# Fourteen groups of context value rows gathered in the experts' first rounds, and a stage border with loads on both sides of it

## The chip, the cores and the metric

One core of one Trainium2 chip runs the whole program as one launch. The metric is the device time of the launch in microseconds (us), the median of several runs. Its engines run side by side and are named as in the profile: PE (TensorE, matrix products; PEld are its weight loads), DVE (VectorE), ACT (ScalarE), POOL (GpSimd, which here mostly issues gathers), and SP (SyncE, which issues the plain transfers). They meet only in semaphores.

## The reference, cut to what matters

One layer of a backbone for 1024 latent tokens and 256 context tokens of width 1024: a mixing half (projection, attention, a gated linear recurrence, output projection), then a product-key expert half, then a norm. The change is in the expert half:

```python
def peer_ffn(x, w_q, sub_keys, u, v):
    q = (x @ w_q).reshape(N, PEER_HEADS, 2, PEER_D_HALF)
    s = jnp.einsum('nhpd,pkd->nhpk', q, sub_keys)
    s_top, i_top = lax.top_k(s, PEER_TOPK)            # 16 of 128, twice per head
    ...                                               # top 16 of the 256 sums, softmax g
    act = jax.nn.gelu(jnp.einsum('cd,ced->ce', x_c, u[e_c]))   # 128 experts per token
    return jnp.einsum('ce,ced->cd', g_c * act, v[e_c])
```

Each token picks 128 of 16384 experts; an expert is one row of u (its key) and one row of v (its value), 4 KB each.

## The kernel before

**Stages.** Tokens are handled in tiles of 128: 8 latent, 2 context. Four latent tiles (the dense tiles) go through all 16384 experts by matrix products. The other four latent tiles and the two context tiles are gathered: for every one of a tile's 128 slots, an indirect DMA from POOL brings one u row per token (128 rows, 512 KB) and DVE takes its dot product with the token; then for every token, the 128 v rows of its slots are gathered and PE sums them with the weights. Four tokens make a *value group*: four gathers of 512 KB and eight products [32 columns of weights x 512] into one PSUM tile; a tile has 32 groups.

The order is: context tiles through mixing and routing; latent mixing, with the context tiles' key dots beside it; **latent routing** (`routing`, names `route_lat_*`), which computes scores and top-k for the 8 latent tiles and has all 64 context value groups beside it (`val_*`); **placing** (`place_weights`), which builds the dense tiles' weight matrix g, token by expert, tile by tile in two SBUF grids of 8 MB and stores each to HBM; the **experts** (`experts`, names `exp_*`); the final norm. Every stage is one block: all engines meet at its end, and the next stage's buffers take the place of the old ones.

**Latent routing.** PE runs over 4 weight slabs x 2 chunks of 512 tokens; a chunk is 4 column tiles of 8 x 2 products, then 16 x 2 short products for the scores of its 4 units. A value group stands after every half column tile (`values(1)`, twice per `ct`), in PE's program order. DVE takes two units at a time in `turn(unit)`, 16 turns; the line that starts a turn's decoding of the last one is L1592. POOL does per two units: `pick` (L1562, a product of 128x1024) and one group of gathers, twice, then `steps` and two groups: four groups, 16 gathers, per turn. Both lists of groups are in POOL's and PE's program order, so a late gather holds all that follows. After the last turn PE turns the gathered tiles' activations (`h_ps`, the PSUM tile the value groups use), ACT stores them, then takes the exponential of the weights (L1528), and DVE norms them (L1734 to L1739).

**Placing.** DVE compares indices with an iota, PE multiplies the one-hot pairs, ACT writes the grid; SP stores each tile's grid when it is full (L1877) and the block ends when the last store has landed. 32 of the first gathered latent tile's key dots stand beside it.

**Experts.** 64 rounds of 2 expert rows: SP loads u (512 KB), v (512 KB) and g (256 KB) for each; ACT and DVE split them in high and low halves; PE makes `a_ps` (48 products of 128x512), then for the round before `o_ps` (48 products), which DVE adds to `acc`. Beside it the four gathered latent tiles: rounds 0 to 7 ("keys") have 12 key gathers each, rounds 8 to 55 ("both") 8 key gathers and 8 value gathers (2 groups), rounds 56 to 63 ("values") 16 value gathers. Key rows sit in a ring of 4, value rows in a ring of two groups. On POOL the gathers alternate, and each waits for its place in the ring. At a tile's end ACT copies the sums out and SP stores them (`finish`). Before round 0 the stage loads h2T (2 MB) and the first two u, and splits them.

**How DVE's round is ordered** (it sets the round's pace where the dots are many):

```python
add_tile(2, DENSE_TILES - 2)
factors(); DOT()
add_tile(2, DENSE_TILES - 1)
factors_turned()
spread()
DOT(); split_v(0)
...
DOT(); add_tile(1, 0); DOT(); add_tile(1, 1)
```

`split_v(0)` waits for v's high half from ACT, and so for the load of v.

## Time and profile before

| | us |
|---|---|
| median of 3 runs | 3849.93 |
| lowest and highest of them | 3842.12, 6262.26 |
| the profiled execution's own time | 3871.46 |
| its span, first to last instruction | 3869.7 |
| latent routing in it, from 1119.7 to 1610.3 | 490.6 |
| placing, from 1610.3 to the last store's issue at 1834.05 | 223.8 |
| that store, to the next stage's first instruction at 1864.89 | 30.8 |
| experts, to 3811; final norm, to 3869.7 | 1946; 58.7 |

Over the span PE is busy 82%, DVE 68%, POOL 52%, ACT 27%; the 16 DMA engines moved 1137.52 MB, 294 GB/s on the mean. Times of a stretch are read from the start of the span. A matrix product of fp32 operands stands as two records in the latent routing's rows. A PE product's duration holds its pipeline's latency, so the spacing of products is less than their duration.

### The profile page before, as it was taken

What the parts mean: (1) busy time and instruction counts of PE and PEld (TensorE: products, weight loads), DVE (VectorE), ACT (ScalarE), POOL (GpSimd) and SP (SyncE); (2) the same over time, 40 slices, a digit from 0 to 9 for tenths busy, and PEclk for the clock granted to TensorE, in tenths of its full rate; (3) what the DMA queues carried; (4) which work ended last, traced back from release to release, by engine and by line L of the source; (5) the groups of instructions that cost most, each with busy time, mean ns of one, the idle gap of its engine ahead of it and who ended that gap; (6) DMA issues with size and microseconds to landing.
All of it is one profiled execution on the core that took longest, in us unless ns stands there. A gap on an engine that the chain in (4) does not pass through costs nothing. (4 is left out here: it accounts for less than half of the span.)

```text
span 3869.7 us, 47496 instructions
## 1 busy us (share of the span) xinstructions
PE 3181.5 (82%) x15280; PEld 2098.8 (54%) x15280; DVE 2635.3 (68%) x5937; ACT 1043.0 (27%) x1811; POOL 2012.7 (52%) x1765
## 2 busy tenths in 40 slices
PE   5776799698969888577377899998999899999993
PEld 3546345465433333366266666666666666666662
DVE  2227687697457777799488777767777777775445
ACT  4431044365110010266222222222222222222221
POOL 0001455354237888421345677767677677775450
PEclk8888899899979999688688999999999999999996
DMA  6522677666578988566887999999999999999996
GB/s 252 183 82 89 229 247 251 189 226 229 207 254 307 330 310 305 195 203 202 302 284 268 387 391 388 382 348 397 370 380 379 372 376 387 384 389 343 343 352 247
DMA packets 412569, 1137.52 MB, mean 294 GB/s; under 512 B 33937, under 2 KB 129425, under 8 KB 412177
## 3 DMA queue, kind: packets, MB, share of 16 engines
q0 software_dynamic: 221184, 805.40, 57.1%
q1 hardware_dynamic: 191248, 330.43, 24.0%
q8 instruction: 69, 1.13, 0.1%
q14 instruction: 68, 0.55, 0.0%
HBM read 1080.13 MB, written 55.58 MB: 293 GB/s over the span
## 5 line engine op out<-in xcount | busy, mean ns | idle before, releaser
L2195 POOL DMA_INDIRECT exp_key_row<-in_u_rows,exp_u_id x480 | 598.2, 1246 | 328.2 <-DVE exp_dot L2249 154.5
L2203 POOL DMA_INDIRECT exp_value_row<-in_v_rows,exp_v_id x512 | 576.6, 1126 | 343.1 <-issue 165.2
L2249 DVE CUSTOM_DVE_ANT_0 exp_key_row<-exp_key_row,exp_x 128x1024 f32<-128x1024 f32 x480 | 585.0, 1222 | 189.4 <-DMA exp_key_row<-in_u_rows,exp_u_id 156.3
L358 POOL DMA_INDIRECT ahead_row<-in_u_rows,keep_expert_id x256 | 328.5, 1283 | 370.7 <-DVE keep_dot L368 309.7
L2112 PE MATMUL exp_o_ps<-exp_v_hi,exp_w_hi 128*128 128x512 f32 x1024 | 346.6, 421 | 160.7 <-DVE exp_acc L2312 153.0
L2097 PE MATMUL exp_a_ps<-exp_xT_hi,exp_u_hi 128*128 128x512 f32 x1024 | 411.5, 402 | 56.8 <-DVE exp_xT_lo L2227 50.5
L2312 DVE TENSOR_TENSOR exp_acc<-exp_o_ps,exp_acc 128x1024 f32<-128x1024 f32 x256 | 311.4, 1222 | 147.7 <-PE exp_o_ps L2112 129.1
L2097 PE MATMUL exp_a_ps<-exp_xT_lo,exp_u_hi 128*128 128x512 f32 x1024 | 404.1, 395 | 0.0
L2097 PE MATMUL exp_a_ps<-exp_xT_hi,exp_u_lo 128*128 128x512 f32 x1024 | 402.0, 393 | 0.0
L368 DVE CUSTOM_DVE_ANT_0 ahead_row<-ahead_row,ahead_x 128x1024 f32<-128x1024 f32 x256 | 304.2, 1221 | 70.1 <-DMA ahead_row<-in_u_rows,keep_expert_id 66.1
L2112 PEld LDWEIGHTS exp_o_ps<-exp_v_hi,exp_w_hi 128*128 128x128 f32 x1024 | 197.4, 201 | 265.7 <-DVE exp_acc L2312 204.0
L434 POOL DMA_INDIRECT val_row<-in_v_rows,keep_value_id x256 | 273.6, 1069 | 115.2 <-issue 68.8
L2112 PE MATMUL exp_o_ps<-exp_v_lo,exp_w_hi 128*128 128x512 f32 x1024 | 333.2, 408 | 0.0
L2112 PE MATMUL exp_o_ps<-exp_v_hi,exp_w_lo 128*128 128x512 f32 x1024 | 331.1, 406 | 0.0
L2097 PEld LDWEIGHTS exp_a_ps<-exp_xT_hi,exp_u_hi 128*128 128x128 f32 x1024 | 194.5, 190 | 148.6 <-DVE exp_xT_lo L2227 50.7
L2083 PE MATMUL exp_v_ps<-exp_value_row,exp_hot 128*32 128x512 f32 x2048 | 248.8, 598 | 10.1 <-DMA exp_value_row<-in_v_rows,exp_v_id 9.5
L1454 PE MATMUL route_lat_q_ps<-mix_featT,route_lat_slab 128*128 128x512 f32 x512 | 238.4, 611 | 2.0 <-DMA route_lat_slab<-in_w_q 2.0
L617 PE MATMUL proj_lat_ps<-mix_featT,proj_lat_slab 128*128 128x512 f32 x512 | 224.9, 598 | 11.0 <-DMA proj_lat_slab<-in_w_in 11.0
L2148 ACT ACTIVATE exp_v_hi<-exp_v_raw 128x1024 fp32r<-128x1024 f32 x128 | 135.0, 1055 | 365.4 <-PE exp_o_ps L2112 214.3
L2112 PEld LDWEIGHTS exp_o_ps<-exp_v_lo,exp_w_hi 128*128 128x128 f32 x1024 | 203.6, 199 | 46.4
L2112 PEld LDWEIGHTS exp_o_ps<-exp_v_hi,exp_w_lo 128*128 128x128 f32 x1024 | 202.9, 198 | 45.6
L2151 ACT ACTIVATE exp_hidden<-exp_a_ps 128x512 f32<-128x512 f32 x128 | 76.5, 598 | 547.5 <-PE exp_a_ps L2097 409.4
(376 smaller groups left out, 5188.1 us busy)
## 6 DMA issues: line engine op xcount, KB each, us to landing
exp_u_raw<-in_uT SPq DMA_DIRECT2D x130, 512.0 KB
exp_v_raw<-in_v_rows SPq DMA_DIRECT2D x128, 512.0 KB
scratch_g<-place_grid SPq DMA_DIRECT2D x4, 8192.0 KB, 35.8
exp_g_raw<-scratch_g SPq DMA_DIRECT2D x128, 256.0 KB
proj_ctx_mod_slab<-in_w_mod SPq DMA_DIRECT2D x8, 2048.0 KB, 14.4
proj_ctx_slab<-in_w_in SPq DMA_DIRECT2D x10, 1024.0 KB, 5.1
proj_lat_slab<-in_w_in SPq DMA_DIRECT2D x10, 1024.0 KB, 7.9
mod_slab<-in_w_mod SPq DMA_DIRECT2D x4, 2048.0 KB, 19.4
```

What stands on the lines that cost most here:

```text
L358: nc.gpsimd.indirect_dma_start(out=ahead.row[:, n % KEY_RING, :], out_offset=None, in_=io["u_rows"], in_offset=bass.IndirectOffsetOnAxis(a ...
L368: nc.vector.tensor_tensor_reduce(out=row, in0=row, in1=ahead.x[:, n // SLOTS - ahead.first, :], scale=1.0, scalar=0.0, op0=ALU.mult, op1=A ...
L434: nc.gpsimd.indirect_dma_start(out=val.row[:, 4 * slot + t, :], out_offset=None, in_=io["v_rows"].rearrange("a b n -> (a b) n"), in_offset ...
L617: last = nc.tensor.matmul(ps[C * (ct % 2) + c][:, 0:width], slab[ct // 2][:, k, ct % 2 * P:(ct % 2 + 1) * P], hT[:, k, g.at + at:g.at + at ...
L1454: last = nc.tensor.matmul(q_ps[ct][:, 0:width], slab[:, a % 2, k, ct * P:(ct + 1) * P], h2T[:, k, g.at + at:g.at + at + width], start=(k = ...
L2083: mm = nc.tensor.matmul(v_ps[QUAD * t:QUAD * (t + 1), half * SLAB:(half + 1) * SLAB], hot[:, i % 2, t, :], value_row[:, 4 * (i % 2) + t, h ...
L2097: mm = nc.tensor.matmul(a_ps[e][:, :], u[part][:, e, k, :], xT[xp][:, k, :], start=(k == 0 and part == 0 and xp == 0), stop=(k == KD - 1 a ...
L2112: mm = nc.tensor.matmul(o_ps[t % 2][:, c, :], w[part][:, 1 - parity, e, t * P:(t + 1) * P], v[xp][:, 1 - parity, e, c * SLAB:(c + 1) * SLA ...
L2195: nc.gpsimd.indirect_dma_start(out=key_row[:, j % RING, :], out_offset=None, in_=io["u_rows"], in_offset=bass.IndirectOffsetOnAxis(ap=u_id ...
L2203: nc.gpsimd.indirect_dma_start(out=value_row[:, 4 * (j % 2) + t, :], out_offset=None, in_=io["v_rows"].rearrange("a b n -> (a b) n"), in_o ...
L2249: nc.vector.tensor_tensor_reduce(out=key_row[:, j % RING, :], in0=key_row[:, j % RING, :], in1=x[:, :], scale=1.0, scalar=0.0, op0=ALU.mul ...
L2312: nc.vector.tensor_tensor(acc[:, t, :], o_ps[t % 2][:, :, :].rearrange("p c n -> p (c n)"), acc[:, t, :], ALU.add).then_inc(added, 1)
```

## The change

Fourteen of the 64 context value groups (the last 14 of the second context tile) leave latent routing and are gathered and summed in the experts' rounds 1 to 7, two per round, where "keys" rounds had no values; POOL's list there becomes key, value, key, value, key, key, value and so on. The context tile's weights stay in `keep["share"]`; at round 1 PE turns them, and after round 7 a new `finish(-1)` copies the sums out and stores the 56 rows.

The border between placing and experts changes too. `acc` becomes a lasting buffer, so that h2T can be loaded into it during placing; x and the first two u are loaded at placing's start; the last grid's store is split into its first 4 expert rows (`g_first`) and the other 124 (`g_rest`), and the block of placing no longer waits for either. SP waits for `g_first` before the first g load, and every engine that writes a buffer lying over the second grid waits for `g_rest` at round 1. Other buffers (routing's rest, two of attention's, the norm's squares, the routes) move onto `acc`; their instructions stay as they are.

```diff
+FIRST_KEYS = 4
+LATE_GROUPS = 14
 class Values:
+        self.units = [(k, q) for k in range(CONTEXT_GATHER) for q in range(self.GROUPS)]
+        del self.units[-LATE_GROUPS:]
 def factor_weigh(nc, keep, val, dve, k):
-    nc.vector.tensor_tensor(val.factor[:, k, :], val.act[:, :], keep["share"][:, k * SLOTS:(k + 1) * SLOTS], ALU.mult)\
+    share = keep["share"][:, k * SLOTS:(k + 1) * SLOTS]
+    nc.vector.tensor_tensor(share, val.act[:, :], share, ALU.mult)\
 def routing(...):  (on PE and on POOL)
-            values_left = [(k, q) for k in range(CONTEXT_GATHER) for q in range(val.GROUPS)] if val else []
+            values_left = list(val.units) if val else []
 def place_weights(nc, io, keep, scratch, routes, ahead, edge):
         def _(sp):
-            sp.dma_start(ahead.x[:, 0, :], scratch["h2"][0]).then_inc(x_in, 16)
+            sp.dma_start(ahead.x[:, 0, :], scratch["h2"][0]).then_inc(edge.x_in, 16)
+            for n in range(2):
+                sp.dma_start(edge.u_raw[:, n, :, :], io["uT"][n]).then_inc(edge.u_in[n], 16)
+            sp.wait_ge(turned, DENSE_TILES)
+            sp.dma_start(keep["acc"][:, :, :].rearrange("p t n -> p (t n)").rearrange("p (k n) -> p k n", k=KD),
+                         scratch["h2T"]).then_inc(edge.h2_in, 16)
-            for t in range(DENSE_TILES):
+            for t in range(DENSE_TILES - 1):
                 sp.wait_ge(placed, (t + 1) * PER_TILE)
                 sp.dma_start(place[:, :, t * P:(t + 1) * P], grid[t % 2][:, :, :]).then_inc(stored[t % 2], 16)
-            for j in range(2):
-                sp.wait_ge(stored[j], 16 * (DENSE_TILES // 2))
+            last = slice((DENSE_TILES - 1) * P, DENSE_TILES * P)
+            sp.wait_ge(placed, DENSE_TILES * PER_TILE)
+            sp.dma_start(place[:, 0:FIRST_KEYS, last], grid[1][:, 0:FIRST_KEYS, :]).then_inc(edge.g_first, 16)
+            sp.dma_start(place[:, FIRST_KEYS:N_KEYS, last], grid[1][:, FIRST_KEYS:N_KEYS, :]).then_inc(edge.g_rest, 16)
+            sp.wait_ge(stored[0], 32)
+            sp.wait_ge(stored[1], 16)
 def experts(nc, io, keep, scratch, ahead, edge):
             with engine.Fori(1, FIRST // 2) as i:
-                body(2 * i, 0, "keys", None, None)
-                body(2 * i + 1, 1, "keys", None, None)
+                body(2 * i, 0, "keys", None, 2 * i + FIRST)
+                body(2 * i + 1, 1, "keys", None, 2 * i + 1 + FIRST)
+            finish(-1)
         def value_groups(r, mode):
-            if mode == "both":
-                return [2 * r - 2 * FIRST + i for i in range(2)]
+            if mode in ("keys", "both") and at_least(r, 1):
+                return [2 * r - 2 + i for i in range(2)]
         def _(sp):
-            sp.dma_start(h2T, scratch["h2T"]).then_inc(h2_in, 16)
...
-            load_u(0, 0)
-            load_u(1, 1)
...
                         sp.wait_ge(weighted, n - 1)
+                    else:
+                        sp.wait_ge(edge.g_first, 16)
+                    if isinstance(r, int) and r == 1:
+                        sp.wait_ge(edge.g_rest, 16)
             def finish(k):
-                sp.wait_ge(out_ready, k + 2)
+                sp.wait_ge(out_ready, k + 3)
+                if isinstance(k, int) and k < 0:
+                    for t in range(4):
+                        rows = slice(QUAD * (t + 1) - LATE_GROUPS, QUAD * (t + 1))
+                        sp.dma_start(scratch["ffn"][CTX.first + 1][rows, :], out[rows, :]).then_inc(late_stored, 16)
         def _(pe):
+                late_tile = mode == "keys" and isinstance(r, int) and r == 1
+                if late_tile:
+                    nc.tensor.transpose(v_ps[:, 0:P], keep["share"][:, SLOTS:2 * SLOTS], keep["ident"][:, :])\
+                      .then_inc(factor_turned, 1)
         (on ACT, POOL and DVE, at the head of their round 1)
+                if isinstance(r, int) and r == 1:
+                    act.wait_ge(edge.g_rest, 16)
         def _(pool):
-                if keys and groups:
-                    moves = [x for pair in zip([("key", j, n, 0) for j, n in enumerate(keys)], moves) for x in pair]
+                for j, n in enumerate(keys):
+                    moves.append(("key", j, n, 0))
+                    if len(keys) == len(values) or j % 3 != 2:
+                        moves += values[0:1]
+                        del values[0:1]
+                moves += values
```

## Rows read from the trace of the kernel before

**Rows 1.** Windows: latent routing, placing, the last store, the experts' start.

```profile
core 0: us, PE busy (x) PEld busy (x) DVE busy (x) ACT busy (x) POOL busy (x), PEclk, DMA share, GB/s
1119.70:1610.30 490.60, 410.14 (x1830) 166.28 (x1830) 329.18 (x1857) 48.85 (x78) 361.57 (x336) 0.92 0.85 298
1610.30:1834.05 223.75, 160.73 (x1036) 153.48 (x1036) 218.02 (x464) 150.72 (x384) 50.75 (x32) 0.83 0.63 191
1834.05:1864.89 30.84, 0.00 (x0) 0.00 (x0) 0.00 (x0) 0.00 (x0) 0.00 (x0) 0.57 0.90 272
```

**Rows 2.** Who waited for whom in latent routing: us, times, longest.

```profile
PE route_lat_h_ps L448 <- DMA val_row<-in_v_rows,keep_value_id: 58.9, 31, 4.9
DVE routes_first L1585 <- POOL route_lat_hit L1562: 48.2, 16, 4.8
```

**Rows 3.** Costliest groups of instructions on POOL in latent routing.

```profile
L434 POOL DMA_INDIRECT val_row<-in_v_rows,keep_value_id x256 | 273.6, 1069 | 115.2 <-issue 68.8 <-PE route_lat_h_ps L448 35.8 <-POOLq L101 8.7
L1562 POOL TENSOR_TENSOR route_lat_hit<-route_lat_hit,route_lat_key_step 128x1024 f32<-128x1024 f32 x32 | 75.8, 2369 | 5.0 <-DVEq L1716 4.5
```

**Rows 4.** Timeline of DVE: the decoding line of turns 12 and 14 and of the tail.

```profile
1481.13 0.18 DVE L1592 TENSOR_SCALAR route_lat_region<-route_lat_best_at 128x64 uint32<-128x64 uint32 x1
...
1536.84 0.18 DVE L1592 TENSOR_SCALAR route_lat_region<-route_lat_best_at 128x64 uint32<-128x64 uint32 x1
...
1585.72 0.20 DVE L1592 TENSOR_SCALAR route_lat_region<-route_lat_best_at 128x64 uint32<-128x64 uint32 x1
```

**Rows 5.** Timeline of PE: the last chunk's first products, one group, its scores.

```profile
1482.83 3.60 PE L1454 MATMUL route_lat_q_ps<-mix_featT,route_lat_slab 128*128 128x512 f32 x8
1486.35 1.95 PE L448 MATMUL route_lat_h_ps<-val_row,val_spread 128*32 128x512 f32 x16
1534.81 3.90 PE L1470 MATMUL route_lat_s_ps<-route_lat_keysT,route_lat_qT 128*128 128x128 f32 x32
```

**Rows 6.** Timeline of the last steps of latent routing and the first of placing.

```profile
1604.02 1.28 ACT L1528 ACT_TABLE_LOAD   x1
1606.40 1.22 DVE L1734 TENSOR_REDUCE route_lat_norm<-routes_weight 128x64 f32<-128x1024 f32 x1 [9.07 <-ACT routes_weight L1528]
1610.47 0.23 DVE L1792 COPY place_mine<-routes_first 128x128 f32<-128x128 f32 x1 [0.54 <-PEq L101]
```

**Rows 7.** Timeline around the border of placing and experts.

```profile
1834.05 0.37 SPq L1877 DMA_DIRECT2D scratch_g<-place_grid  x1
1864.89 0.19 POOL L2178 COPY exp_u_id<-keep_expert_id 128x12 int32<-128x12 int32 x1 [59.63 <-POOLq L101]
1876.75 1.06 ACT L2130 ACTIVATE exp_u_hi<-exp_u_raw 128x1024 fp32r<-128x1024 f32 x1 [42.73 <-DMA exp_u_raw<-in_uT]
1889.33 1.23 DVE L2249 CUSTOM_DVE_ANT_0 exp_key_row<-exp_key_row,exp_x 128x1024 f32<-128x1024 f32 x1
1891.62 1.22 DVE L2219 TENSOR_TENSOR exp_v_lo<-exp_v_raw,exp_v_hi 128x1024 fp32r<-128x1024 f32 x1
```

**Rows 8.** DMA issues: count, KB each, median us from issue to landing.

```profile
scratch_g<-place_grid SPq DMA_DIRECT2D x4, 8192.0 KB, 35.8
route_lat_keysT<-in_keysT SPq DMA_DIRECT2D x1, 128.0 KB, 17.6
```

**Rows 9.** Windows of the experts: rounds 3 to 5, round 8, rounds 9 to 22.

```profile
1987.23:2080.49 93.26, 72.02 (x290) 58.10 (x289) 77.23 (x109) 19.75 (x27) 47.53 (x40) 0.89 0.82 287
2144.31:2177.67 33.36, 27.89 (x130) 20.16 (x129) 21.90 (x30) 6.71 (x9) 21.17 (x20) 0.90 1.03 407
2177.67:2579.82 402.15, 377.11 (x1794) 270.97 (x1793) 303.68 (x420) 90.34 (x126) 290.58 (x253) 0.97 1.00 383
```

**Rows 10.** Key gathers in rounds 3 to 5; value products in rounds 11 and 12.

```profile
L2195 POOL DMA_INDIRECT exp_key_row<-in_u_rows,exp_u_id x37 | 46.9, 1269 | 46.8 <-DVE exp_dot L2249 40.2 <-issue 4.0 <-POOL exp_u_id L2178 2.7
L2083 PE MATMUL exp_v_ps<-exp_value_row,exp_hot 128*32 128x512 f32 x64 | 7.8, 598 | 0.0
```

**Rows 11.** Windows: rounds 7 to 9 and rounds 23 to 25, each with a tile's end.

```profile
2113.39:2203.71 90.32, 78.49 (x355) 58.73 (x354) 69.58 (x100) 19.76 (x27) 62.09 (x53) 0.92 0.96 363
2579.82:2670.78 90.96, 82.25 (x387) 59.44 (x386) 65.27 (x92) 20.42 (x28) 59.01 (x52) 0.94 0.96 363
```

More of the change, by code:

```diff
@@ L351, in hold, with __init__ @@
         self.first = first
+class Edge:
+    def __init__(self, scope, signals):
+        self.u_raw = scope.sb("u_raw", [P, 2, KD, P])
+        self.u_id = scope.sb("u_id", [P, 2, KEYS_PER_ROUND], I32)
+        self.dot = scope.sb("dot", [P, 2, KEYS_PER_ROUND])
+        self.act_row = scope.sb("act_row", [P, SLOTS])
+        self.h2_in = signals.sem("edge_h2_in")
+        self.u_in = [signals.sem(f"edge_u_in{n}") for n in range(2)]
+        self.x_in = signals.sem("edge_x_in")
+        self.g_first = signals.sem("edge_g_first")
+        self.g_rest = signals.sem("edge_g_rest")
 def gather_keys(nc, io, ahead, pool, n):
@@ L414, in factor_turn @@
     pe.wait_ge(val.factor_ready, k + 1)
[L415 removed]
+    nc.tensor.transpose(ps[:, 0:P], keep["share"][:, k * SLOTS:(k + 1) * SLOTS], keep["ident"][:, :])\
+      .then_inc(val.turned, 1)
 def factor_spread(nc, val, act, k, ps):
@@ L1362, in routing @@
         score = s.sb("score", [P, SCORE_RING, 4, N_KEYS])
-        rest = s.sb("rest", [P, 2, 4, N_KEYS])
+        rest = keep["acc"][:, 3, :].rearrange("p (x c n) -> p x c n", x=2, c=4)
         top = s.sb("top", [P, 2, 4, TOPK])
@@ L1536, in _ @@
         def _(pool):
-            values_left = [(k, q) for k in range(CONTEXT_GATHER) for q in range(val.GROUPS)] if val else []
+            values_left = list(val.units) if val else []
             def values(count):
@@ L1740, in _, with place_weights @@
             c.wait()
-def place_weights(nc, io, keep, scratch, routes, ahead):
+def place_weights(nc, io, keep, scratch, routes, ahead, edge):
     first, second, weight = routes
@@ L1929, in experts @@
         zeroed = s.sem("zeroed")
-        u_in = [s.sem(f"u_in{n}") for n in range(2)]
+        u_in = edge.u_in
         v_in = [s.sem(f"v_in{n}") for n in range(2)]
@@ L2029, in load_u @@
                 sp.dma_start(u_raw[:, e, :, :], io["uT"][n]).then_inc(u_in[e], 16)
-            load_u(0, 0)
-            load_u(1, 1)
             def body(r, parity, mode, tile, _):
-                if tile is not None and mode in ("keys", "both"):
-                    if mode == "both":
-                        sp.wait_ge(dots, SLOTS * tile + RING)
-                    sp.dma_start(x[:, :], scratch["h2"][tile]).then_inc(x_in, 16)
+                if tile is not None and mode == "both":
+                    sp.wait_ge(dots, SLOTS * tile + RING)
+                    sp.dma_start(x, scratch["h2"][tile]).then_inc(x_in, 16)
                 if mode == "end":
@@ L2174, in body @@
                     return
+                if isinstance(r, int) and r == 1:
+                    pool.wait_ge(edge.g_rest, 16)
                 c = Chain(pool, own_pool)
@@ L2180, in body @@
                 if groups:
-                    c.step(nc.gpsimd.tensor_copy(v_id[:, parity, 0:4 * len(groups)],
-                                                 keep["value_id"][:, bass.ds(4 * groups[0] + BASE, 4 * len(groups))]))
+                    c.step(nc.gpsimd.tensor_copy(
+                        v_id[:, parity, 0:4 * len(groups)],
+                        keep["value_id"][:, bass.ds(4 * groups[0] + BASE - 4 * LATE_GROUPS, 4 * len(groups))]))
                 c.wait()
@@ L2237, in body @@
                 new_tile = tile is not None and (not isinstance(tile, int) or tile) and mode != "end"
+                late_tile = mode == "keys" and isinstance(r, int) and r == 1
                 last = mode == "end"
@@ L2272, in spread @@
                     i, m = groups.pop(0)
-                    per = 2 if mode == "both" else 4
+                    per = 4 if mode == "values" else 2
                     q = per * local + i
                     if new_tile and i == 0:
-                        dve.wait_ge(factorT_ready, tile)
+                        dve.wait_ge(factorT_ready, tile + 1)
+                    if late_tile and i == 0:
+                        dve.wait_ge(factorT_ready, 1)
                     dve.wait_ge(values_done, m + 1)
@@ L2313, in add_tile @@
                                                 acc[:, t, :], ALU.add).then_inc(added, 1)
+                if isinstance(r, int) and r == 1:
+                    dve.wait_ge(edge.g_rest, 16)
                 DOT = dot_product
@@ L2467, in program @@
+        with Scope(nc, "edge") as e:
+            edge = Edge(e, s)
+            ahead.hold(e, CONTEXT_GATHER, 1)
+            place_weights(nc, io, keep, scratch, routes, ahead, edge)
+            experts(nc, io, keep, scratch, ahead, edge)
         final_norm(nc, io, scratch)
```

156 lines of the change are left out of this document (78 added, 78 removed).

## The prediction

> **What bounds the kernel now.** I read first the windows by stage, then within a stage who waits for whom, then the timeline at the places the change touches. The chain that ended last covers only the final norm and says nothing here.
>
> In latent routing no engine is full: PE 410, POOL 362, DVE 329 of 490.6 us [rows 1]. The reader is to see that POOL's time is larger than its busy share. A gather is 1.07 us and another 0.30 of issue gap (68.8 us in 228 waits) [rows 3]. Per turn that is 16 x 1.37 = 21.9, two picks of 2.37, and about 1.1 of small steps: 27.7 us, against two turns in 55.7 us (1481.13 to 1536.84) [rows 4]. So POOL's gathers set the pace; PE waits 58.9 us for value rows in its program order, and DVE waits 48.2 us for picks that stand behind gathers [rows 2]. Placing is DVE alone, 218 of 223.75 us [rows 1]. Then all five engines rest 30.8 us for one store [rows 1], and another 24.4 us pass until the first key dot at 1889.33 [rows 7]. In the experts' keys rounds (31.1 us each) DVE is busy 25.7 us, DMA 0.82 at 287 GB/s; in the both rounds (28.7 us each) DMA is full, 1.00 at 383 GB/s [rows 9]. The keys rounds are thus the ones with room, but not much.
>
> **Latent routing: -30 us.** Groups go out three ahead and four per turn, so 50 groups end in turn 11 (3 + 4 x 12 = 51). PE takes 8 per chunk in chunks 1 to 6 and the last 2 in chunk 7, so up to 1481 nothing changes. From turn 12 on POOL has only picks. DVE's busy time is 329/16 = 20.6 us per turn; I take 20.7 with no wait for POOL. PE must deliver the last chunk in time: 8 x 3.6 + 2 x 1.95 = 32.7 us from 1482.83 [rows 5], so its scores come at about 1517 instead of 1536, while DVE wants them at 1481.1 + 41.4 = 1522.5. PE is no longer late. Four turns take 82.8 instead of 104.6 us (1481.13 to 1585.72) [rows 4]: -21.8. At the end, PE's value groups and the transposes behind them no longer hold ACT until 1604.02: DVE waited 9.07 us for ACT's exponential [rows 6]; what stays of it is a table load of 1.28 and the exponential of 1.1 behind DVE's last weights, of which DVE covers 1.5 with the ids. -8. Together -30, range -24 (some POOL wait stays, PE at a lower clock) to -33. Late next is DVE itself. The removed PE products, 14 x 1.95 us, lay in the same wait and are not counted twice.
>
> **Placing: 0.** Three loads more on SP's queue (3 MB) and the gathers of the first key rows meet in its first 15 us; DVE is the bound and reaches its first dot 10 us in. If the first row came late it would cost up to 3 us once. The second store of a tile is another 0.37 us on SP. The end wait is for stores that were issued a whole tile earlier (56 us; a store takes 35.8 [rows 8]), so it is free.
>
> **The border: -23 us.** Experts start about 1 us after 1834.4 instead of at 1864.89. u and h2T are there, so ACT splits at 1835.5 instead of 1876.75, and DVE reaches its first dot 12.6 us later, as before [rows 7]: 1848 for 1889.33, which would be -41. But DVE's third step is split_v, and v's load is issued by SP behind the 7.75 MB of g_rest. Do loads of one queue go past each other? The nearest row: keysT, 128 KB, landed 17.6 us after its issue with 2 MB of slabs issued just before it on the same queue [rows 8]. So I take it that they don't. The store takes 30.8 to 35.8 us in this kernel [rows 1, 8], the four key rows (2.1 MB) share its engines; v lands at about 1869.5, DVE goes on at 1871 for 1891.62: -21, and its key rows wait ready, which saves 2 more. The waits for g_rest at round 1 are by then met. Behind the waiting DVE stand dots, and POOL's ring of 4 waits for them; PE has done both first `a_ps` and waits for the next u, also in that queue. Ends: -15 if the key rows take half the engines' time for long, -41 if v comes past.
> The Trainium skill says in "DMA: Bandwidth & Descriptors", section "Queues, rings and completion order", that an engine consumes a ring's descriptors in order and goes round between the queues by packets. By that rule the SP loads stay behind the store and only POOL's gathers come through; the trace's 17.6 us agree, and the sum stays at -23.
>
> **Rounds 1 to 7: +21 us.** Per round are added 8 gathers of 512 KB, two weight builds on DVE (under 1 us), and two groups on PE (7.8/4 = 1.95 us each) [rows 10]. PE and DVE have it free: 25.7 + 0.7 us of DVE, 24 + 3.9 of PE. The round's bytes grow from 8.5 to 12.5 MiB = 13.1 MB. At the 383 GB/s of the full rounds that is 34.2 us against 31.1: +3.1, times 7 = +21. POOL's queue is near: 20 gathers at 1.269 + 0.30 is 31.4, with copies and their waits 34. Ends: round 8 shows 407 GB/s [rows 9], so 32.2 us, +8; with waits of POOL for value places, 37 us, +40.
> The Trainium skill, same page, section "Where 436 GB/s comes from", gives about 358 GB/s as what binds a core's traffic with HBM. By it a round would be 36.6 us and this term +38, the whole -11. Here the trace differs: 383 GB/s over 402 us [rows 9], so the sum goes by the row.
>
> **The tile's end at round 8: +4 us.** finish(-1) puts before SP's loads of round 8 a wait for ACT's copy, which waits for PE's last value group, at the end of PE's round. Queued behind it are x, v, g and u of round 8. Before, SP waited there for the dots only. Rounds 7 to 9 took 90.3 us; rounds 23 to 25, with such a finish, 91.0 [rows 11], where three both rounds are 86.1: +4.9 for a full tile's end, against 90.3 - (31.1 + 57.4) = 1.8 now. +3, and a little for a queue fuller than at 23; ends 0 and +11 (how much later PE's last group is than the last dot). Rounds 8 to 63 keep their work: 0. The final norm: 0; the context rows are there earlier than it needs them.
>
> **Sum.** -30 - 23 + 21 + 4 = -28 against the profiled execution's own 3871.5: 3843.5. That execution is 21.5 us above the median of 3849.9; taken over to it, 3822. Two per cent is 77 us, about what a measurement of this kernel can tell from no change: the case is small against it.
>
> **The rivals.**
> *Value gathers make POOL's list the bound of the keys rounds.* A value gather waits for its ring place, which PE frees only in its `o_ps` phase; keys for DVE's dots stand behind it, DVE runs dry. For it: 34 us of POOL in a 34 us round, and POOL's and DMA's limits meet. Against: in both rounds the same alternation holds 28.7 us with DMA full. With two waits of 2.7 us in a round 39.3 us: +57, the tile's end +11; -30 - 23 + 68 = +15, 3865, slower than before. It decides from a round of 38 us (49 us in 7 rounds).
> *The loads come past the store.* Round 0 runs at once, -41 for -23: 3804. For it: nothing in the rows; against: the 17.6 us.
> *The rounds absorb the gathers* at 32.2 us: +8 for +21: 3809.
> *The rounds move their bytes at a lower rate* than the full rounds, 36.6 us each: +38 for +21, 3839. Against: the full rounds' 383 GB/s [rows 9]. The 358 GB/s of the Trainium skill's page, cited above, would do this.
> *The routing gains only its tail*, DVE's turns staying at the 27 us of now because picks or scores bind otherwise: -8 for -30, 3844. Against: 48.2 us of waits for POOL.
>
> **How the numbers follow.** Forecast 0.5, POOL's list 0.12, loads past the store 0.08, absorbed 0.16, lower rate 0.06, routing tail 0.08. The range takes in the absorbed rounds with part of the border's better end, and up to near the first rival: 3790 to 3858. Faster by over 2% (under 3773) needs all good ends and more: 0.04. Slower by over 2% (over 3927) needs a rival of twice its price: 0.02.
>
> **What would show it.** Value gathers on POOL end near turn 11; L1592's last four spacings near 21 us; placing starts 30 us earlier and lasts 224 us. The last store is followed at once by experts; ACT's first v split about 35 us after it (forecast) or at once (rival). Rounds 1 to 7 near 34 us with DMA near 1.0 and DVE's waits for key rows grown; at 38 or more, with POOL waiting for PE, the first rival. Wrong would also be a longer placing, or rounds after 10 that changed.

## The result, and the profile after

The changed kernel took 3788.12 us (median of 4 runs, 3784.38 to 3792.11), the kernel before beside it 3846.02: a ratio of 0.9851, 95% interval 0.983 to 0.9871. That is 58 us less, where 28 were forecast. The profiled execution of the changed kernel took 3790.08 us, with a span of 3788.3. The ratio leaves out one run of the kernel before, at 6262.26 us.

The windows of the changed kernel by stage: latent routing, placing, the experts' rounds 2 to 6, rounds 10 to 21.

```profile
core 0: us, PE busy (x) PEld busy (x) DVE busy (x) ACT busy (x) POOL busy (x), PEclk, DMA share, GB/s
1132.70:1591.70 459.00, 371.64 (x1610) 156.22 (x1611) 333.61 (x1867) 48.52 (x78) 298.94 (x281) 0.92 0.72 255
1591.70:1816.20 224.50, 162.88 (x1034) 156.39 (x1032) 217.03 (x455) 151.35 (x384) 49.36 (x32) 0.81 0.66 204
1926.60:2101.60 175.00, 139.98 (x642) 101.14 (x641) 131.69 (x190) 32.31 (x46) 119.27 (x111) 0.89 0.99 374
2197.30:2522.30 325.00, 314.67 (x1538) 226.09 (x1537) 259.03 (x362) 77.53 (x108) 234.59 (x216) 1.00 1.03 406
```

The first three are near what was reckoned with. The fourth is not: against the both rounds of before [rows 9] the same work moves at 406 GB/s for 383, and TensorE's granted clock is 1.00 for 0.97.

To see where the time went I cut both traces at the same events: the first slab load of latent routing, the load of x, the last store's issue, and the first `exp_hidden` of round 0, 8 and 56. In us:

| stretch | before | after | difference |
|---|---|---|---|
| latent routing | 492.1 | 459.1 | -33.0 |
| placing | 221.6 | 224.5 | +2.9 |
| last store to round 0 | 58.4 | 40.2 | -18.2 |
| rounds 0 to 7 | 251.8 | 282.5 | +30.7 |
| rounds 8 to 55 | 1402.1 | 1325.6 | -76.5 |
| rounds 56 to 63 and the end | 323.3 | 323.9 | +0.6 |

All that the forecast spoke of comes to -17.6. The rest, a stretch that was put at zero, is four times as much. (Before latent routing, after's execution is 12.4 us later than that of before. That is scatter: an experiment with before's buffers, e2, is 7.2 us later there, and the changed kernel profiled once more, e12, 0.8 us.) The -76.5 is too large for the kernels' difference: the profiled execution of before was 25 us above its median. Another kernel with before's order, e1 below, has 1362.4 us in rounds 8 to 55, in an execution 10 us below its median. What the order is worth is therefore taken from medians, further down.

**At the border**, the timeline of the changed kernel: SP's queue, then ACT and DVE.

```profile
1816.22 0.51 SPq L1907 DMA_DIRECT2D scratch_g<-place_grid  x1
...
1817.52 1.06 ACT L2167 ACTIVATE exp_u_hi<-edge_u_raw 128x1024 fp32r<-128x1024 f32 x1 [1.74 <-PEq L2096]
1817.78 31.89 SPq L2069 DMA_DIRECT2D exp_v_raw<-in_v_rows  x1
...
1849.72 1.13 SPq L2076 DMA_DIRECT2D exp_g_raw<-scratch_g  x1
...
1855.41 1.06 ACT L2187 ACTIVATE exp_v_hi<-exp_v_raw 128x1024 fp32r<-128x1024 f32 x1 [30.20 <-DMA exp_v_raw<-in_v_rows]
...
1856.50 1.22 DVE L2269 TENSOR_TENSOR exp_v_lo<-exp_v_raw,exp_v_hi 128x1024 fp32r<-128x1024 f32 x1 [23.96 <-ACT exp_v_hi L2187]
```

The splits of u run at once after the store's issue, 41 us earlier after it than in [rows 7], and then all wait for v, as forecast. v does not only land late: the instruction that issues its load stands 31.89 us on SP, behind the store, with no wait for a semaphore of the kernel ahead of it. The store landed 36.0 us after its issue, v's load 37.6 us after its own.

**In the both rounds** the page of each kernel has the clue. Of before, TensorE's output products and DVE's adds (busy us, mean ns | idle time before them and what ended it):

```profile
L2112 PE MATMUL exp_o_ps<-exp_v_hi,exp_w_hi 128*128 128x512 f32 x1024 | 346.6, 421 | 160.7 <-DVE exp_acc L2312 153.0
...
L2312 DVE TENSOR_TENSOR exp_acc<-exp_o_ps,exp_acc 128x1024 f32<-128x1024 f32 x256 | 311.4, 1222 | 147.7 <-PE exp_o_ps L2112 129.1
```

The same of the changed kernel:

```profile
L2149 PE MATMUL exp_o_ps<-exp_v_hi,exp_w_hi 128*128 128x512 f32 x1024 | 338.0, 412 | 83.6 <-DVE keep_acc L2364 83.3
...
L2364 DVE TENSOR_TENSOR keep_acc<-exp_o_ps,keep_acc 128x1024 f32<-128x1024 f32 x256 | 311.4, 1220 | 108.1 <-PE exp_o_ps L2149 107.4
```

TensorE's idle time ahead of its output products falls from 160.7 to 83.6 us. Such a wait is seen in the timeline of before, round 10:

```profile
2214.41 1.94 PE L2083 MATMUL exp_v_ps<-exp_value_row,exp_hot 128*32 128x512 f32 x16
...
2217.04 1.23 DVE L2249 CUSTOM_DVE_ANT_0 exp_key_row<-exp_key_row,exp_x 128x1024 f32<-128x1024 f32 x1 [1.10 <-DMA exp_key_row<-in_u_rows,exp_u_id]
...
2218.20 1.21 DVE L2312 TENSOR_TENSOR exp_acc<-exp_o_ps,exp_acc 128x1024 f32<-128x1024 f32 x1
2219.47 0.74 PE L2112 MATMUL exp_o_ps<-exp_v_hi,exp_w_hi 128*128 128x512 f32 x2 [3.12 <-DVE exp_acc L2312]
...
2221.58 1.22 DVE L2249 CUSTOM_DVE_ANT_0 exp_key_row<-exp_key_row,exp_x 128x1024 f32<-128x1024 f32 x1 [2.16 <-DMA exp_key_row<-in_u_rows,exp_u_id]
```

The windows of before around it (columns as above):

```profile
2214.00:2216.00 2.00, 2.00 (x19) 0.53 (x17) 1.95 (x4) 0.00 (x0) 2.00 (x3) 1.00 1.02 399
2216.00:2218.00 2.00, 0.35 (x4) 0.00 (x0) 0.96 (x1) 0.00 (x0) 1.09 (x2) 1.00 1.03 419
2218.00:2220.00 2.00, 0.53 (x2) 0.48 (x3) 1.42 (x3) 0.00 (x0) 1.41 (x2) 1.00 1.03 409
2220.00:2222.00 2.00, 2.00 (x8) 1.54 (x8) 0.42 (x1) 0.00 (x0) 1.40 (x2) 0.73 1.03 412
2222.00:2224.00 2.00, 1.77 (x5) 0.85 (x3) 2.00 (x4) 0.21 (x1) 1.68 (x2) 0.50 1.03 406
2224.00:2226.00 2.00, 2.00 (x8) 1.70 (x9) 2.00 (x2) 0.00 (x0) 1.70 (x2) 0.91 1.02 401
```

The reader is to see a chain. DVE waits for a key row; behind its dot stands the add that frees `o_ps`; TensorE waits for that add; after this pause its granted clock falls from 1.00 to 0.50 (2.4 to 1.2 GHz) and returns some 4 us later; all that TensorE frees comes late. The key row's lateness looks small (1.1 and 2.16 us) and stands in DVE's waits only; TensorE waits 3.12 us, because the dot (1.23) and the add (1.21) come after it.

In before, 14 of the 48 rounds take 26.04 us and most of the others 28 to 34 us; in the changed kernel 34 take 26.5 to 27.3. Two neighbouring rounds of before, and one of the changed kernel:

```profile
2234.88:2260.92 26.04, 26.04 (x130) 18.82 (x129) 21.60 (x30) 6.46 (x10) 18.10 (x16) 1.00 1.01 381
2260.92:2290.61 29.69, 26.36 (x130) 18.74 (x129) 21.84 (x30) 6.46 (x9) 21.32 (x21) 1.00 1.02 405
2251.99:2278.93 26.94, 26.16 (x130) 18.84 (x129) 21.58 (x30) 6.47 (x10) 19.51 (x18) 1.00 1.03 409
```

TensorE is busy through the whole of the 26.04 us, at the granted clock 1.00, as in all 14 of them: that is its own work in a both round. The changed kernel's round is 0.9 us above that. Over rounds 8 to 55 TensorE's idle time falls from 108.7 to 60.7 us, and its busy time for the same products from 1293.4 to 1264.9. That second part, 28 of the 76 us, is an estimate of what the lower clock costs; the ends of products are modelled in a trace, so it is a rough one.

What put the key rows earlier is the last piece of the change. The line that builds POOL's list, `if len(keys) == len(values) or j % 3 != 2`, is asked anew for each key, while `values` shrinks. In rounds 8 to 55, where there are 8 of each, the lengths are equal at the first key only; after that `j % 3` decides, and every third key has no value behind it: K V K V K K V K V K K V K V V V, for strict pairs K V K V before. The timeline of POOL in the changed kernel shows a part of it, key, value, key, key, value, L2245 for keys, L2253 for values:

```profile
2240.20 0.93 POOL L2245 DMA_INDIRECT edge_row<-in_u_rows,edge_u_id  x1 [0.30 <-issue]
2241.44 0.94 POOL L2253 DMA_INDIRECT exp_value_row<-in_v_rows,exp_v_id  x1 [0.30 <-issue]
2242.68 0.94 POOL L2245 DMA_INDIRECT edge_row<-in_u_rows,edge_u_id  x1 [0.31 <-issue]
2243.93 0.94 POOL L2245 DMA_INDIRECT edge_row<-in_u_rows,edge_u_id  x1 [0.30 <-issue]
2245.17 0.94 POOL L2253 DMA_INDIRECT exp_value_row<-in_v_rows,exp_v_id  x1 [0.30 <-issue]
```

### The profile page after: what moved, and what is told of

Its sections match the earlier page's. It is cut to its first block and busy times, and to the rows that moved or that the text cites. A ratio compares the mean times of both kernels' runs of the same rounds, so it can differ in the third digit from the quotient of the medians.

```text
span 3788.3 us, 47442 instructions
## 1 busy us (share of the span) xinstructions
PE 3158.0 (83%) x15281; PEld 2086.8 (55%) x15281; DVE 2639.1 (70%) x5952; ACT 1044.5 (28%) x1812; POOL 1958.1 (52%) x1772
## 5 line engine op out<-in xcount | busy, mean ns | idle before, releaser
L2253 POOL DMA_INDIRECT exp_value_row<-in_v_rows,exp_v_id x568 | 711.9, 1253 | 273.5 <-issue 177.7
L2300 DVE CUSTOM_DVE_ANT_0 edge_row<-edge_row,edge_x 128x1024 f32<-128x1024 f32 x480 | 583.5, 1218 | 277.5 <-DMA edge_row<-in_u_rows,edge_u_id 242.9
L2245 POOL DMA_INDIRECT edge_row<-in_u_rows,edge_u_id x480 | 511.1, 1065 | 354.0 <-DVE edge_dot L2300 204.8
L2149 PE MATMUL exp_o_ps<-exp_v_hi,exp_w_hi 128*128 128x512 f32 x1024 | 338.0, 412 | 83.6 <-DVE keep_acc L2364 83.3
L2364 DVE TENSOR_TENSOR keep_acc<-exp_o_ps,keep_acc 128x1024 f32<-128x1024 f32 x256 | 311.4, 1220 | 108.1 <-PE exp_o_ps L2149 107.4
L2149 PE MATMUL exp_o_ps<-exp_v_lo,exp_w_hi 128*128 128x512 f32 x1024 | 324.2, 398 | 0.0
L2149 PE MATMUL exp_o_ps<-exp_v_hi,exp_w_lo 128*128 128x512 f32 x1024 | 321.3, 395 | 0.0
L2120 PE MATMUL exp_v_ps<-exp_value_row,exp_hot 128*32 128x512 f32 x2272 | 278.1, 601 | 40.5 <-DMA exp_value_row<-in_v_rows,exp_v_id 40.4
L2149 PEld LDWEIGHTS exp_o_ps<-exp_v_hi,exp_w_hi 128*128 128x128 f32 x1024 | 188.6, 193 | 192.3 <-DVE keep_acc L2364 145.7
L456 POOL DMA_INDIRECT val_row<-in_v_rows,keep_value_id x200 | 208.8, 1044 | 100.5 <-issue 55.6
L2190 ACT ACTIVATE exp_hidden<-exp_a_ps 128x512 f32<-128x512 f32 x128 | 76.5, 598 | 568.9 <-PE exp_a_ps L2134 568.9
## 6 DMA issues: line engine op xcount, KB each, us to landing
scratch_g<-place_grid SPq DMA_DIRECT2D x3, 8192.0 KB, 35.8
```

Source lines behind the costliest of these rows:

```text
L456: nc.gpsimd.indirect_dma_start(out=val.row[:, 4 * slot + t, :], out_offset=None, in_=io["v_rows"].rearrange("a b n -> (a b) n"), in_offset ...
L2120: mm = nc.tensor.matmul(v_ps[QUAD * t:QUAD * (t + 1), half * SLAB:(half + 1) * SLAB], hot[:, i % 2, t, :], value_row[:, 4 * (i % 2) + t, h ...
L2149: mm = nc.tensor.matmul(o_ps[t % 2][:, c, :], w[1 - parity][part][:, e, t * P:(t + 1) * P], v[1 - parity][xp][:, e, c * SLAB:(c + 1) * SLA ...
L2245: nc.gpsimd.indirect_dma_start(out=key_row[:, j % RING, :], out_offset=None, in_=io["u_rows"], in_offset=bass.IndirectOffsetOnAxis(ap=u_id ...
L2253: nc.gpsimd.indirect_dma_start(out=value_row[:, 4 * (j % 2) + t, :], out_offset=None, in_=io["v_rows"].rearrange("a b n -> (a b) n"), in_o ...
L2300: nc.vector.tensor_tensor_reduce(out=key_row[:, j % RING, :], in0=key_row[:, j % RING, :], in1=x, scale=1.0, scalar=0.0, op0=ALU.mult, op1 ...
```

## The experiments

All are compared with runs of the kernel before on the same chip. They ran on four chips, which gave before 3846.4 (e1 to e4), 3888.1 (e5 to e8), 3846.8 (e9 to e12) and 3872.1 us (e13 to e15), so ratios are set side by side, not times. The last four columns come from one profiled execution each: us a round over rounds 8 to 55, from the events above, the others between 2100 and 3450 us. They are to be compared on one chip, or between the first and the third: a kernel with the new order has 27.6 us a round there and 28.59 on the second chip (e5).

| | order, edit | ratio, interval | us a round | TensorE waits for adds | clock | GB/s |
|---|---|---|---|---|---|---|
| before | pairs | 1 | 29.21 | 105.0 in 35 | 0.96 | 377 |
| after | new | 0.9851, 0.983 to 0.9871 | 27.62 | 34.7 in 14 | 0.99 | 398 |
| e1 | after, pairs | 0.9951, 0.9934 to 0.9968 | 28.38 | 86.6 in 44 | 0.98 | 390 |
| e2 | before, new order | 0.9903, 0.9867 to 0.9939 | 27.64 | 43.0 in 15 | 0.99 | 396 |
| e3 | after, no group moved | 0.985, 0.9817 to 0.9883 | 27.55 | 31.3 in 10 | 0.99 | 398 |
| e4 | after, store waited for | 0.9848, 0.9817 to 0.9879 | 27.67 | 35.7 in 13 | 0.99 | 398 |
| e5 | after, loads first | 0.9827, 0.9806 to 0.9849 | 28.59 | 60.4 in 24 | 0.98 | 386 |
| e6 | after, one swap | 1.0003, 0.9983 to 1.0024 | 29.88 | 114.1 in 33 | 0.95 | 371 |
| e7 | after, keys far ahead | 1.0094, 1.0071 to 1.0118 | 30.77 | 6.0 in 1 | 0.94 | 359 |
| e8 | after, second key early | 0.9861, 0.9842 to 0.9881 | 28.90 | 71.9 in 32 | 0.97 | 383 |
| e9 | e1, adds first | 0.9822, 0.9788 to 0.9857 | 27.66 | 34.5 in 9 | 0.99 | 398 |
| e10 | after, one key ahead | 0.9829, 0.9784 to 0.9874 | 27.54 | 54.9 in 43 | 0.99 | 399 |
| e11 | e3, adds first | 0.9847, 0.981 to 0.9884 | 27.88 | 22.6 in 5 | 0.99 | 395 |
| e12 | after again | 0.9832, 0.9794 to 0.9869 | 27.68 | 38.2 in 15 | 0.99 | 397 |
| e13 | before, adds first | 0.9899, 0.9883 to 0.9916 | 28.92 | 70.5 in 22 | 0.97 | 383 |
| e14 | e15, loads first | 0.9819, 0.9801 to 0.9836 | 28.84 | 57.0 in 22 | 0.97 | 386 |
| e15 | e10, adds first | 0.9853, 0.9832 to 0.9873 | 28.45 | 52.7 in 18 | 0.98 | 388 |

**e1: the changed kernel with strict pairs again.**

```diff
+                paired = len(keys) == len(values)
...
-                    if len(keys) == len(values) or j % 3 != 2:
+                    if paired or j % 3 != 2:
```

> The kernel after, with POOL's gathers in rounds 8 to 55 in strict pairs again (key, value, key, value), as before the change; all else as after. Theory 1 (the order of POOL's list makes rounds 8 to 55 faster, 27.6 against 29.2 us each): the rounds go back to 28.7 to 29.2 us, the whole to 3835 to 3860 us. Theory 2 (where the buffers lie in SBUF makes them faster): the rounds stay at 27.6 us, the whole at 3788.

3827.8 us: 0.9951. This is the change that was reckoned, and it is worth 19 us, where the forecast had 28. The order is worth about 1% more, 39 us; theory 2, the buffers' places, falls. The total stayed just under the range expected (3835 to 3860), and so did the rounds (28.38 for 28.7 to 29.2).

e1's trace shows more: strict pairs are not slow in every round. Up to the first tile's end of the both rounds they keep the pace of the new order, after it they lose it, and rounds of 26.04 and of 28 to 31 us alternate. Rounds 16 to 22 of e1 (columns as above):

```profile
2355.60:2544.34 188.74, 184.41 (x898) 131.18 (x897) 150.66 (x210) 45.26 (x64) 142.50 (x126) 1.00 1.03 408
```

Rounds of 26.5 to 27.3 us number 1 of 48 in before, 12 in e1, 32 in e2 and 34 in the changed kernel. The order makes such rounds the rule; it does not create them.

**e2: the kernel before with the new order alone.** The loop of the changed kernel in place of `zip` in rounds 8 to 55.

> The kernel before, with nothing changed but POOL's order in rounds 8 to 55: key, value, key, value, key, key, value, key, value, key, key, value, key, value, value, value. Theory 1 (order): these rounds fall to about 27.6 us each, the whole from 3846 to 3775 to 3800. Theory 2 (places of buffers): 3846, no change. The stretch before latent routing shows whether the 12 us that the kernel after loses there belongs to its buffers (then routing starts at 1120 here) or to the execution.

3804.89 us: 0.9903. The order gives the same 1% from the other side, without moved groups and without new buffers: 27.64 us a round. (The total is 5 us above the 3775 to 3800 expected.)

**e3: the changed kernel with no group moved.** `LATE_GROUPS = 0`, and rounds 1 to 7 without values, `finish(-1)` and their waits.

> The kernel after, with no groups moved: all 64 in latent routing, none in rounds 1 to 7, no copy of sums after round 7; the border and POOL's order as after. By the traces of before and after the move gives 31 us in latent routing and costs 31 us in rounds 0 to 8: so 3788, within 8 us, with latent routing at 490 us again and rounds 1 to 7 at 31 us. By my prediction's terms (gain 30, cost 25) it would be 3793. If the gathers also disturb the rounds after 8, it is under 3780.

3785.39 us: 0.985, the same as the changed kernel. Its trace has latent routing at 491.2 us and rounds 0 to 7 at 252.7, as before: what moving the 14 groups takes out of routing (-32 or so) the early rounds pay back (+30). Moved or not, no difference is measured.

**e4: the last store waited for, early loads kept.**

```diff
+            sp.wait_ge(edge.g_first, 16)
+            sp.wait_ge(edge.g_rest, 16)
```

> The kernel after, with placing's block waiting for both parts of the last store as before; x, u and h2T are still loaded early. The overlap of the store with the experts' start is then gone, the early loads stay. By the trace of after, round 0's first Gelu comes 40.6 us behind the store's issue; with the wait the store (31 us), 1 us, the splits and 21 us of products come one after another, near 52: +10 to +14, so 3800. If early loads were all of the gain it stays 3788; if the overlap is all, 3806.

3790.23 us: 0.9848. From the last store to round 0 it takes 45.6 us, the changed kernel 40.2, before 58.4. So by these traces, of the border's 18 us 13 come from the loads of u and h2T that lie in placing, and 5 from working beside the store; the medians (3790.23 for 3788.12) don't tell the two kernels apart. I had put more on the second.

**e5: v, g and u of round 0 and 1 ahead of the rest of the last store** in SP's program order.

> The kernel after, with the store of the last grid's other 124 expert rows issued by SP only behind round 0's loads of v, g and u. Theory: what held round 0 in the kernel after was SP's issue of the first v load, 31.9 us long behind that store, and not the store's share of the DMA engines. Then the first Gelu comes near 20 us behind the first part's store instead of 40, round 0 runs at once, and round 1 waits for the store at its head: 15 to 20 us less up to round 2, the whole 3768 to 3775. Rival (the store's bytes are the limit wherever they stand): what round 0 gains round 1 waits, 3788.

3823.09 us: 0.9827, the interval (0.9806 to 0.9849) overlaps that of the changed kernel. Round 0's first Gelu comes 15.8 us after the issue of the store's first part, for 40.6 in the changed kernel (the rest is issued 9.9 us behind the first part, for 0.4 there), but round 1 waits for it: SP's next load of v is held 31.05 us behind it. From the start of placing to round 8 it is 542.0 us, for 547.2. The store is not hidden, it is met one round later. Of the loads' moved place at most some 5 us stay.

**e6, e7, e8: other orders in rounds 8 to 55 of the changed kernel.** The numbers 1a to 1d in the expectations are guesses, made before TensorE's waits were read, at why the order counts.

```diff
+                if mode == "both":
+                    ks, vs = [m for m in moves if m[0] == "key"], [m for m in moves if m[0] == "value"]
+                    moves = [(ks if c == "K" else vs).pop(0) for c in "KVKVKVKVKVKVKKVV"]
```

(e6; in e7 "KKVKKVKKVKKVVVVV", in e8 "KKVVKVKVKVKVKVKV".)

> The kernel after, in rounds 8 to 55 the list key, value in pairs for 13 places, then key, key, value, value: only the last key goes ahead of one value. Theory 1a (key rows asked for late in the round make DVE wait, so every key moved ahead helps): a little of the way, rounds of 28.2 us, the whole 3815. Theory 1b (the strict pairs have a state of their own that any disturbance at the list's end breaks): 27.6 us, 3788. Theory 1c (the end of the list doesn't matter): 3828 as the strict pairs.

> The kernel after, in rounds 8 to 55 the list key, key, value four times, then key, key for the last time with the values behind: key key value key key value key key value key key value value value value value. Theory 1a (keys ahead): 27.6 us or less per round, 3788 or less. Rival (value rows then come late for PE, whose program order they hold): above 28.5 us, over 3825.

> The kernel after, in rounds 8 to 55 the list key, key, value, value, then strict pairs to the end. Theory 1d (the first value gather waits for PE's last use of its ring place, and the second key behind it comes late): with one key more ahead of that wait the rounds go to 27.6 us, 3788. If it is the late keys and not the early ones that count (1a): near the strict pairs, 3820 to 3828.

3890.24, 3927.73 and 3837.81 us: 1.0003, 1.0094 and 0.9861. Of the guesses, 1a fails in e7, and 1b and 1c in e6. 1d's total (3788 us, a ratio of 0.985) is near e8's 0.9861; its 27.6 us a round is not, but on this chip e5, with the new order, has 28.59 as well. All three have the border's gain too, so they are to be held against e1's 0.9951 (from another chip): e8's order gains 0.9%, those of e6 and e7 lose 0.5% and 1.4%. So "keys earlier" has an optimum. In e7 TensorE hardly waits for adds, but for value rows; who waited for whom on PE in e7, 2100 to 3450 us (total, times, longest):

```profile
PE exp_v_ps L2120 <- DMA exp_value_row<-in_v_rows,exp_v_id: 140.7, 43, 10.9
PE exp_o_ps L2149 <- DVE keep_acc L2367: 6.0, 1, 6.0
```

A pause for value rows goes with a low clock too, 0.94. e8 gains although only its second key stands earlier; e6, whose last key stands earlier, does not. That the late keys are the ones that count is thus not shown; which place in the list counts for how much, these orders do not settle.

**e9: strict pairs as in e1, and on DVE each of the last two adds of a round ahead of the dot before it.** This is the test of the chain. POOL's list in the both rounds is that of before; only what stands behind a late key row on DVE is changed, in the rounds 0 to 7 too.

```diff
-                DOT(); add_tile(1, 0); DOT(); add_tile(1, 1)
+                add_tile(1, 0); DOT(); add_tile(1, 1); DOT()
```

> The changed kernel with strict pairs again in rounds 8 to 55 (as e1), and on DVE each of the last two output adds of a round put ahead of the dot that stood before it. Theory (2a), formed on the traces so far: in strict pairs the rows of keys 6, 7 and 0 come late, DVE waits for them, the add of an output tile stands behind that dot in DVE's order, PE waits for the add (105.0 us in 35 waits between 2100 and 3450 us of the kernel before, 34.7 in 14 after the change), its granted clock falls to 0.50, and what it frees comes late. Then the swap alone gives strict pairs most of what the new order gives: rounds 8 to 55 at 27.0 to 27.8 us, PE's waits for DVE's adds in that stretch under 55 us, mean clock 0.99 or more, ratio to before 0.984 to 0.990. Rival (2b), the order in which row gathers stand in the DMA queue is itself what moves more bytes: no change against e1, 28.2 to 28.8 us a round, ratio 0.993 to 0.998. Rival (2c), DVE's adds then wait for PE and hold the dots and POOL's ring of key rows: 29 us or more a round, ratio over 1.0.

3778.05 us: 0.9822, against 0.9951 of e1 (on another chip, where before has the same median); rounds of 27.66 for 28.38 us, which is 34.5 us of the 38.8 between the two traces, and 35 of 48 rounds at 26.5 to 27.3. Who waited on PE, 2100 to 3450 us, in e1:

```profile
PE exp_o_ps L2149 <- DVE keep_acc L2365: 86.6, 44, 8.8
```

And in e9:

```profile
PE exp_o_ps L2149 <- DVE keep_acc L2365: 34.5, 9, 8.8
PE exp_v_ps L2120 <- DMA exp_value_row<-in_v_rows,exp_v_id: 31.8, 39, 1.1
```

DVE meanwhile waits more for key rows than in e1 (197.9 for 132.6 us). So DVE's longer waits did not cost time once the add no longer stood behind them. The rival that the order in the DMA queue itself moves more bytes falls: here pairs move 398 GB/s. So does the one that the adds hold the dots.

**e10, e11, e12 beside it on the same chip**: each key one place ahead, "KKVKVKVKVKVKVKVV"; e3 with the adds first; the changed kernel again.

> The changed kernel with the order K K V K V K V K V K V K V K V V in rounds 8 to 55: each key one place ahead of strict pairs all the way through, against one key ahead over the first five places in e8, one at the very end in e6, and up to two in the changed kernel. By (2a) what counts is that keys 6 and 7 are ahead without starving the values: 27.0 to 27.8 us a round, ratio 0.983 to 0.989, mean clock 0.99. If two places are needed for the last keys: 28 to 28.9 us a round, ratio 0.990 to 0.996, like e1. If a value tail of two is what spoils e6 (1.0003): 29.5 us or more, ratio near 1.0.

> e3 (all 64 groups in latent routing, border overlap, the new order in rounds 8 to 55) with DVE's last two adds of a round ahead of the dots, in the keys rounds too. By (2a) the keys rounds have no such stall at 31 us and the rounds from 8 on are at 27.6 us already, where DMA's 406 GB/s is the bound: within 8 us of e3, ratio 0.981 to 0.986. If PE's remaining 31.3 us of waits for adds are on the path, up to 20 us better: ratio 0.979. By (2c) 20 to 60 us worse.

> The changed kernel again, unedited, on this chip, beside the other three: 0.983 to 0.9871 as first measured. It says how far the ratios of kernels run on different chips can be set side by side; if it comes out beyond 0.981 or 0.990, ratios from different calls are compared only roughly.

3770.95 (0.9829), 3786.52 (0.9847) and 3778.18 us (0.9832, 0.9794 to 0.9869). e10 is the fastest median of this chip, though not apart from the changed kernel there. In e11 the adds-first edit on top of the new order adds nothing: 0.985 and 0.9847. That fits order and adds removing the same wait. But it is a sum of two parts: against e3, rounds 0 to 7 took 245.6 us for 252.7, where I expected nothing, and rounds 8 to 55 took 1338.1 for 1322.6, with 50.4 us of TensorE's waits for value rows between 2100 and 3450 us for 27.3.

**e13: the kernel before with the adds first, nothing else.**

> The kernel before, unedited but for DVE's two adds ahead of the dots that stood before them. Theory (2a): the loss lay in the kernel before, so this alone gives what the changed kernel gives: rounds 8 to 55 at 27.5 to 28.0 us for 29.2, PE's waits for DVE's adds between 2100 and 3450 us under 60 us for 105.0, ratio 0.982 to 0.990. Rival (3a): the late dots only hurt together with the moved groups or the other buffers of the changed kernel: 28.8 us a round or more, ratio 0.995 to 1.0.

3834.42 us: 0.9899, interval 0.9883 to 0.9916, the same 1% as e2 has from the order. By the ratio the loss lay in the kernel before, and one line of DVE's order recovers it. By the round, 28.92 us and 70.5 us of waits, the expectation was not met: in this execution, 16 us above its median, the stalls came back after 3000 us, where it moves 372 GB/s for 399 between 2600 and 3000. Nor is all of the gain in the both rounds: rounds 0 to 7 took 244.8 us for 251.8 in before, as in e11. By these traces some 7 of the 38 us come from there.

**e14 and e15**: one key ahead with the adds first, in e14 with the loads of e5 too.

> The changed kernel with the order of e10 (each key one place ahead), the adds first, and the first loads ahead of the rest of the last store (e5). If the three add up: 27.4 us a round, 5 us less up to round 8 (e5 came to round 8 542 us after placing began, the changed kernel after 546 to 547), ratio 0.978 to 0.982. If order and adds are one and the same gain: 0.980 to 0.984, within 8 us of e10. Over 0.986 if the loads ahead of the store cost more in the rounds than they give at the border.

> As e14 without the moved loads. By (2a) the order and the adds remove the same wait, and DMA's 406 GB/s sets 26.95 us from there: ratio 0.981 to 0.985, rounds at 27.4 to 27.7 us. If PE's remaining 54.9 us of waits in e10 still cost time: 27.0 to 27.3 us, ratio 0.977 to 0.981.

3803.85 (0.9819, 0.9801 to 0.9836) and 3815.9 us (0.9853, 0.9832 to 0.9873), rounds of 28.84 and 28.45 us. Rounds of 27.4 to 27.7 were expected. The two edits do not add up beyond either alone, and on this chip both kept part of the stalls (57.0 and 52.7 us of waits for adds). The loads ahead of the store may be worth 12 us by these medians; the intervals touch. From placing's start to round 8 e14 took 531.7 us, e15 542.3. No version is shown to be faster than e9 or e10, which beat the kernel before by 1.7 to 1.8%.

## Why the prediction was wrong

**The step that failed** is "Rounds 8 to 63 keep their work: 0". Their work is the same; their order is not. I read the changed list code as strict pairs wherever keys and values are 8 each, as if the new order were that of rounds 1 to 7 only, and did not run its condition through with a list that shrinks. Shown: the order alone is worth 1.0% (e2 against before, e1 against after), 40 to 42 us by the medians. Without it the forecast's 28 stands against 19 measured, inside its range. Shown too is the way it works: with pairs kept and the adds taken from behind the dots, TensorE's waits for them fall from 86.6 to 34.5 us and the rounds from 28.38 to 27.66 (e9); e13 bears it out by its ratio. Why the key rows come late in pairs, and why just these orders help, stays open. That the fall of the clock carries a part of the loss, some 28 us in the pair of traces by TensorE's busy time, is argued from rows, not isolated; no run kept the clock up through the pause. The Trainium skill, "TensorE: Matmul & The Clock Gate", section "HAM oscillation — how this bites in real kernels", describes a matmul kernel that goes to the lower clock again after each wait for data; the windows of before agree, 0.50 after a pause.

Even with the order seen, the sum would have missed it. I wrote that DMA is full in those rounds, 1.00 at 383 GB/s, and took 383 for its limit. A share of 1.00 was not a limit: the changed kernel moves 406 at 1.03, and round 8 of before had 407 [rows 9]. The 0.97 of the clock beside it was a sign of pauses that I passed over. Nor is 406 shown to be DMA's limit. It is a round's 11.0 MB over the round's time, and of the 26.95 us TensorE's own work is 26.04 to 26.2; beside it stand TensorE's waits for value rows, 42 between 2100 and 3450 us, 27.4 us in all and 1.0 at most.

The other steps, against their terms:
- **Latent routing**, -30: -33.0. Four turns took 79.7 us (1494.09 to 1573.83) for the 82.8 forecast and 104.6 of [rows 4]. The mechanism held.
- **Placing**, 0: +2.9. Traces with the loads in placing have 221.7 to 225.2 us, the three without (before, e2, e13) 221.2 to 222.8: about 2 us, inside the 3 that were allowed for a late first row.
- **The border**, -23: -18.2. The mechanism held, the loads stay behind the store, with SP's issue itself held 31.89 us. Mis-sized: v's split came 39.2 us after the last store's issue, for 35 forecast, and by e4's trace working beside the store gives only 5.
- **Rounds 1 to 7 and the tile's end**, +21 and +4: +30.7. Rounds 2 to 6 took 34.1 to 35.8 us, for 34.2, round 7 before the tile's end 37.3, and round 1 grew most, from 39.2 to 45.8; DMA was at 0.99 and 374 GB/s in rounds 2 to 6, the rate 2% under the 383 of the sum. POOL waited 27.6 us for dots in rounds 2 to 6, and its waits there show none for value places, so the rival of POOL's list did not come. The term's mechanism held, its size was a little larger.
- **The rivals**: loads past the store, rounds absorbed, a lower rate and the routing's tail did not happen. None of them spoke of rounds 8 to 55, which is why the range ended 2 us short of the time. The signs of being wrong did name them: "rounds after 10 that changed" is what came.

Moving the groups, by itself the aim of the change, is worth nothing measurable (e3): it takes 32 us off latent routing, where POOL was the bound, and gives back 30 in rounds 0 to 7, where DMA is at 0.99. The 19 us that e1 keeps are the border's.

On the rate, the rule of 358 GB/s that the prediction cited does not bind here; the Trainium skill's "HBM Reference", section "Specifications (TRN2)", has also that a core streaming alone measures well above that share, about 425 GB/s. With one core running, the 398 to 406 GB/s of the both rounds lie above the share and under that figure.

## What to carry to other kernels

Where an engine waits for data in the middle of its program, ask what stands behind it: an add that frees another engine's buffer belongs ahead of a dot that may be late, and one such swap was worth as much here (0.9899) as the order of the gathers (0.9903); the two together were worth no more. A DMA share of 1.00 with a granted clock of 0.97 beside it was no limit here; look for the fastest round in the same trace, and for what is busy all through it, before a rate is taken as the bound. And run a changed loop's conditions through by hand for every mode that uses it, above all where it consumes the list that it tests.

## What the runs showed that I had not expected

- SP's instruction for a 512 KB load behind the 7.75 MB store on the same queue stood 31.89 us (31.05 in e5 and 30.94 in e14, where a load came behind the store likewise); most other issues of the experts on SP take 0.33 to 0.8 us.
- Both a rate of 383 and one of 406 GB/s show as a DMA share of 1.00 to 1.03 in windows of 300 us and more.
- Strict pairs have fast rounds too: seven in a row at 408 GB/s in e1, and in before 14 in which TensorE never rests, 26.04 us each.
- One kernel can keep more or fewer of the stalls within an execution, and the kernels on the two chips where before is slower kept more: e1 lost the fast pace at a tile's end, e13 moved 399 GB/s between 2600 and 3000 us and 372 between 3000 and 3400. What tips it stays open.
